# Overflow passes of two experts each in the MoE half of a two-layer decoder kernel, with the last group split the same way

## The reference

```python
def hier_moe(h, w_group, b_group, w_expert, b_expert, w_e_gate, w_e_up, w_e_down):
    t = h.reshape(-1, d)
    g_idx = jnp.argmax(t @ w_group + b_group, axis=-1)
    g_w = jnp.take_along_axis(jax.nn.softmax(g_logits, axis=-1), g_idx[:, None], axis=-1)
    e_in = jnp.take_along_axis(e_logits, g_idx[:, None, None], axis=1)[:, 0]
    top_v, top_i = lax.top_k(e_in, TOP_K)                      # TOP_K = 2 of 4
    top_w = jax.nn.softmax(top_v, axis=-1) * g_w
    hid = jax.nn.silu(jnp.einsum('td,edf->tef', t, w_e_gate)) * jnp.einsum('td,edf->tef', t, w_e_up)
    out = jnp.einsum('tef,efd,te->td', hid, w_e_down, combine.astype(t.dtype))
```

## Time and profile before

| | |
|---|---|
| median of 3 runs | 784.68 us |
| profiled execution | 784.63 us |
| its span, first to last instruction | 782.9 us |
| mean granted clock of TensorE (share of full) | 0.999 |
| PE busy | 772.4 us, 99% |
| DVE busy | 646.9 us, 83% |
| ACT busy | 508.1 us, 65% |
| moved by DMA | 186.76 MB |

### The profile page before, as it was taken

The page is one execution under the profiler, slowest core; times in us unless marked ns, Lnnn a source line. Parts: engine busy times, 40 slices in busy tenths (PEclk is TensorE's granted clock), DMA queues, the critical chain, the costliest instruction groups (busy, mean ns, idle before and its releaser), DMA issues.

```text
span 782.9 us, 13142 instructions
## 1 busy us (share of the span) xinstructions
PE 772.4 (99%) x4850; PEld 690.5 (88%) x4850; DVE 646.9 (83%) x847; ACT 508.1 (65%) x592; POOL 22.6 (3%) x36
## 2 busy tenths in 40 slices
PE   8999999999999999999999999999999999999997
PEld 7899999999878888888889999999988888888885
DVE  5868898469689999897874799757968998989895
ACT  7625646655588778786643655565569877878772
POOL 4020000000000000000001000000000000000000
PEclk9999999999999999999999999999999999999999
DMA  9867254266719999998365624526562999999971
GB/s 303 273 215 241 83 201 137 94 216 216 269 54 328 346 383 335 386 338 276 119 214 204 225 97 173 162 72 239 212 234 90 334 365 386 336 363 352 354 262 54
DMA packets 79499, 186.76 MB, mean 239 GB/s; under 512 B 12470, under 2 KB 24408, under 8 KB 79448
## 3 DMA queue, kind: packets, MB, share of 16 engines
q1 hardware_dynamic: 79448, 186.08, 67.0%
HBM read 185.01 MB, written 1.05 MB: 238 GB/s over the span
## 4 chain that ended last, share of the span: by engine, by line
PE 96%; DVE 1%; ACT 1%; DMA 1%; issue 1%; POOL 0%; DVEq 0%; SPq 0%; ACTq 0%; POOLq 0%
PE bank L1380 28%; PE bank L1382 28%; PE bank L1381 28%; PE bank L1774 2%; PE bank L1685 2%; PE bank L1800 1%; PE bank L1662 1%; PE bank L1539 1%; DMA x<-in_x 1%; PE bank L1445 1%; PE bank L1448 0%; PE bank L1560 0%; PE bank L1564 0%; PE bank L1655 0%; PE bank L1769 0%
## 5 line engine op out<-in xcount | busy, mean ns | idle before, releaser
L839 DVE TENSOR_TENSOR w_lo<-raw,w_hi 128x2048 fp32r<-128x2048 f32 (+1 forms) x144 | 313.5, 2197 | 56.4 <-ACT w_hi L522 55.8
L522 ACT ACTIVATE w_hi<-raw 128x2048 fp32r<-128x2048 f32 (+1 forms) x144 | 264.1, 1844 | 135.3 <-PE bank L1382 131.4
L1380 PE MATMUL bank<-a_hi,w_hi 128*128 128x256 f32 x688 | 195.8, 285 | 0.6 <-DVE a_lo L905 0.6
L1381 PE MATMUL bank<-a_hi,w_lo 128*128 128x256 f32 x688 | 194.6, 283 | 0.0
L1382 PE MATMUL bank<-a_lo,w_hi 128*128 128x256 f32 x688 | 194.6, 283 | 0.0
L1380 PE MATMUL bank<-w_hi,y_lo 128*128 128x512 f32 x432 | 170.9, 395 | 0.0
L1382 PE MATMUL bank<-w_lo,y_lo 128*128 128x512 f32 x432 | 168.6, 390 | 0.0
L1380 PEld LDWEIGHTS bank<-a_hi,w_hi 128*128 128x128 f32 x688 | 131.9, 192 | 1.6 <-issue 1.5
L1381 PEld LDWEIGHTS bank<-a_hi,w_lo 128*128 128x128 f32 x688 | 132.0, 192 | 0.1
L1382 PEld LDWEIGHTS bank<-a_lo,w_hi 128*128 128x128 f32 x688 | 132.0, 192 | 0.0
L1381 PE MATMUL bank<-w_hi,y_hi 128*128 128x512 f32 x288 | 112.3, 390 | 0.0
(11 more groups left out here) (309 smaller groups left out, 970.4 us busy)
## 6 DMA issues: line engine op xcount, KB each, us to landing
raw<-in_w_e_gate SPq DMA_DIRECT2D x63, 512.0 KB, 4.9
raw<-in_w_e_up SPq DMA_DIRECT2D x63, 512.0 KB, 6.5
raw<-in_w_gate SPq DMA_DIRECT2D x56, 512.0 KB, 4.5
mid<-in_w_e_down SPq DMA_DIRECT2D x54, 512.0 KB, 6.1
raw<-in_w_in SPq DMA_DIRECT2D x32, 512.0 KB, 6.6
raw<-in_w_e_down SPq DMA_DIRECT2D x18, 512.0 KB, 5.0
raw<-in_w_branch SPq DMA_DIRECT2D x16, 512.0 KB, 4.1
raw<-in_w_o SPq DMA_DIRECT2D x16, 512.0 KB, 4.4
```

Source lines behind the costliest of these rows:

```text
L522: a.activation(w_hi[:, at.part(n), 0:w], raw_at(slot)[:, 0:w], ACT.Copy).then_inc(hi_done, 1)
L839: v.tensor_tensor(w_lo[:, part, 0:w], raw_at(slot)[:, 0:w], w_hi[:, part, 0:w].bitcast(F32), ALU.subtract).then_inc(split_done, 1)
L1380: mm(ps, a2[0], b2[0], start=first, stop=False, skip_group_check=shared)
L1381: mm(ps, a2[1], b2[0], start=False, stop=False, skip_group_check=shared)
```

## The change: half passes for the overflow and for the fourth group

A **half pass** serves two experts of a group (6 units, `units_h`). Groups 0 to 2 keep full passes. Then come the half passes: those for an overflow, if there is one, then experts 12 and 13 of the fourth group, and last, written out, experts 14 and 15. All counters stay as for a full pass: a half pass adds what is missing (`SKIP`) at one of its units.

The tokens of the second 128 whose two best experts are the first two of their group form a class of their own, and are ranked behind all other tokens of the group. DVE finds the class from the expert logits, PE ranks with two masks (`ca`) instead of one, and counts twice: all tokens of the group, and those outside the class. If the first count is over 128, a half pass with the group's experts 0 and 1 is added; if the second is, another with 2 and 3.

Each unit of a half pass is loaded by four DMAs of 256 KB instead of two of 512 KB, with contiguous runs of 2 KB instead of 4 KB. Passes 1 and 2 are written out on PE, ACT and DVE, and the loop runs over half passes. The diff, cut to its core:

```diff
+    units_h = [("gu", 0, 0), ("gu", 0, 1), ("gu", 1, 0), ("gu", 1, 1), ("down", 0, 0), ("down", 1, 0)]
+    PART_H = (0, 1, 2, 3, 1, 2)
+    SKIP = NM - len(units_h)
...
+            return PART_H[n] if self.half else n % PART
+
+        def counted(self, n):
+            return self.unit(n) + 1 + (SKIP if self.half else 0)
+
+        def count(self, n):
+            return 1 + SKIP if self.half and n == 0 else 1
...
+            def load_half(at, l, e0):
+                for n, (kind, i, h) in enumerate(units_h):
+                    slot = at.raw(n)
+                    sp.wait_ge(split_done, at.free(n, False))
+                    dst = raw_at(slot)
+                    for j in range(2):
+                        for q in range(2):
+                            o = 1024 * j + 512 * q
+                            if kind == "gu":
+                                d = dst[:, o:o + 512].rearrange("p (c f) -> p c f", c=2)
+                                w = (w_e_gate, w_e_up)[j]
+                                s = w[l, e0 + i].rearrange("(p c) f -> p c f", c=KT)[:, 4 * h + 2 * q:4 * h + 2 * q + 2, :]
+                            else:
+                                d = dst[:, o:o + 512]
+                                s = w_e_down[l, e0 + i, P * j:P * j + P, 512 * q:512 * q + 512]
+                            sp.dma_start(d, s).then_inc(landed[slot], 16)
...
-                npass = sp.value_load(tab[0:1, 0, 6:7], min_val=NG, max_val=NG + 1)
-                with sp.Fori(NG - 1, npass) as p:
-                    g = sp.value_load(tab[0:1, 0, bass.ds(p, 1)], min_val=0, max_val=NG - 1)
-                    at = At(l, before + p, True)
-                    for n, (kind, i, h) in enumerate(units_m):
-                        load(at, n, kind, i, h, l, g * EPG + i)
-
+                lastp = sp.value_load(tab[0:1, 0, 7:8], min_val=NG, max_val=MAXP - 1)
+                with sp.Fori(NG - 1, lastp) as p:
+                    e0 = sp.value_load(tab[0:1, 1, bass.ds(p, 1)], min_val=0, max_val=NE - 2)
+                    load_half(At(l, before + p, True, True), l, e0)
+                load_half(At(l, before + lastp, True, True), l, NE - 2)
+                npass = sp.value_load(tab[0:1, 0, 8:9], min_val=NG + 1, max_val=MAXP)
...
+                def half_pass(at, PP, tile_next, next_slot, final):
...
+                    hi(at, 3)
+                    silu(0)
+                    hi(at, 4, at.unit(0) + PART + 2)
+                    hidden(0)
+                    hi(at, 5, at.unit(0) + PART + 3)
+                    silu(1)
+                    if not final:
+                        pass_tokens(0, next_slot)
+                        pass_tokens(1, next_slot)
+                        act.wait_ge(S("sil_done"), EPG * PP + EPG)
+                        a.activation(rcur, rslot[:, tile_next], ACT.Copy).then_inc(S("rcur_done"), 1)
+                    if not final or l < DEPTH - 1:
+                        hi(ahead, 0, at.unit(0) + PART + 1)
+                    hidden(1)
+                    if not final or l < DEPTH - 1:
+                        hi(ahead, 1, at.unit(0) + PART + 5)
+                    result(at, PP)
+                    if not final:
+                        hi(ahead, 2, at.unit(0) + PART + NM)
 
...
+                lastp = act.value_load(tab[0:1, 0, 7:8], min_val=NG, max_val=MAXP - 1)
+                expert_pass(At(l, before + 1, True), before + 1, slice(2, 3), 2 * P, False)
+                tile_next = act.value_load(tab[0:1, 0, 3:4], min_val=0, max_val=NG - 1)
+                expert_pass(At(l, before + 2, True), before + 2, bass.ds(tile_next, 1), tile_next * P, False, True)
+                with act.Fori(NG - 1, lastp) as p:
+                    tile_next = act.value_load(tab[0:1, 0, bass.ds(p + 1, 1)], min_val=0, max_val=NG - 1)
+                    half_pass(At(l, before + p, True, True), before + p, bass.ds(tile_next, 1), tile_next * P, False)
+                half_pass(At(l, before + lastp, True, True), before + lastp, None, None, True)
...
-                    step.do(v.tensor_reduce(gm[:, t:t + 1], lg[:, t, 0:NG], AX, ALU.max))
+                    best = step.mark(v.tensor_reduce(gm[:, t:t + 1], lg[:, t, 0:NG], AX, ALU.max))
+                    if t:
+                        e_t = lg[:, t, NG:NR].rearrange("p (g e) -> p g e", g=NG)
+                        step.mark(v.tensor_tensor(cl[:, 0, :], e_t[:, :, 2], e_t[:, :, 3], ALU.max))
+                        step.mark(v.tensor_tensor(cl[:, 1, :], e_t[:, :, 0], e_t[:, :, 1], ALU.min))
+                    step.upto(best)
                     step.do(v.scalar_tensor_tensor(out=r4[:, 0, t, :], in0=lg[:, t, 0:NG], scalar=gm[:, t:t + 1],
...
+                    step.mark(v.tensor_reduce(r1[:, 1, t:t + 1], r4[:, 0, t, :], AX, ALU.max))
+                    if t:
+                        step.mark(v.tensor_tensor(cl[:, 2, :], cl[:, 1, :], cl[:, 0, :], ALU.is_ge))
+                        step.mark(v.tensor_tensor(cl[:, 3, :], cl[:, 0, :], cl[:, 1, :], ALU.is_gt))
+                    step.upto(step.n)
+                    if t:
+                        for i in range(2):
+                            v.scalar_tensor_tensor(out=ca[:, NG * i:NG * i + NG], in0=r4[:, 0, t, :], scalar=r1[:, 1, t:t + 1],
...
+                        dve.wait_ge(S("class_done"), T * (l + 1))
+                        step.do(v.tensor_tensor(r8, small_ps[:, RANK[t]:RANK[t] + 2 * NG], ca, ALU.mult))
+                        step.do(v.tensor_reduce(rk[:, t:t + 1], r8, AX, ALU.add))
...
+                    step.do(v.tensor_tensor(cnt[:, 0, :], cnt[:, 0, :], cnt[:, 1, :], ALU.add))
+                    step.do(v.tensor_scalar(cnt[:, 2:4, :], cnt[:, 0:2, :], float(P), None, ALU.is_gt))
+                    step.mark(v.tensor_reduce(tab_f[:, 1, 8:9], cnt[:, 2:4, :].rearrange("p i g -> p (i g)"), AX, ALU.add))
...
+                def half_pass(at, PP, tile, tile_next, weights, final):
...
+                    lo(at, 3)
+                    hidden(0)
+                    lo(at, 4)
+                    hidden_lo(0)
+                    lo(at, 5)
+                    hidden(1)
+                    if not final:
+                        pass_low(PP, 0, tile_next)
+                        pass_low(PP, 1, tile_next)
+                    hidden_lo(1)
+                    if not final or l < DEPTH - 1:
+                        lo(ahead, 0)
+                    dve.wait_ge(S("scattered"), PP)
+                    v.tensor_scalar(sel_t, posb[:, :], icol[:, tile], None, ALU.is_equal)
+                    if not final:
+                        lo(ahead, 1)
+                    result_lo(PP)
+                    if not final:
+                        lo(ahead, 2)
...
+                    ps = bank[small_bank][:, RANK[t]:RANK[t] + NG + NG * t]
+                    if t:
+                        pe.wait_ge(S("class_done"), T * (l + 1))
+                        mm(ps[:, 0:NG], ones[:, :], ca[:, NG:2 * NG], start=False, stop=False, skip_group_check=True)
+                    else:
+                        pe.wait_ge(S("goh_done"), T * l + 1)
+                    mm(ps, below[:, :], ca if t else r4[:, 3, 0, :], start=False, stop=True,
                        skip_group_check=True).then_inc(S("rank_done"), 1)
 
                 def count():
...
+                def half_pass(at, PP):
...
+                    def down(e, n):
+                        ready(at, n)
+                        pe.wait_ge(S("hd_lo_done"), EPG * PP + 2 * e + 2)
+                        wp = parts(at, n, "p (c m) -> p c m", c=FT)
+                        for h in range(2):
+                            if e and h:
+                                last.then_inc(S("y_bank"), 1)
+                            for f in range(FT):
+                                last = three(bank[4 + h][:, :], both(HD_, e, f), both(wp, f, slice(512 * h, 512 * h + 512)),
+                                             e == 0 and f == 0, e == 1 and f == FT - 1)
+                        last.then_inc(unit_used, 1 + SKIP if e else 1)
+
+                    gate_up(0, 0, 0)
+                    gate_up(0, 1, 1)
+                    gate_up(1, 0, 2)
+                    hidden_tp(0)
+                    gate_up(1, 1, 3)
+                    pe.wait_ge(S("selt_done"), PP)
+                    down(0, 4)
+                    hidden_tp(1)
+                    for i in range(4):
+                        last = scatter(i)
+                    last.then_inc(S("scattered"), 1)
+                    down(1, 5)
...
-                npass = pe.value_load(tab[0:1, 0, 6:7], min_val=NG, max_val=NG + 1)
-                with pe.Fori(1, npass) as p:
-                    expert_pass(At(l, before + p, True), before + p, False)
+                lastp = pe.value_load(tab[0:1, 0, 7:8], min_val=NG, max_val=MAXP - 1)
+                npass = pe.value_load(tab[0:1, 0, 8:9], min_val=NG + 1, max_val=MAXP)
+                expert_pass(At(l, before + 1, True), before + 1, False)
```

(40 more changed lines are left out.)

198 lines of the change are left out of this document (112 added, 86 removed).

## The result

The changed kernel took **773.55 us** in the median of four runs (772.57 to 774.75), the kernel before 784.77 on the same chip (784.68 to 787.08): a ratio of 0.985, 95% interval 0.984 to 0.987. The forecast was 772.9 us with a range of 771.4 to 777.5.

The account below looks back on a forecast made before the run. TensorE, busy 99% of the span and 96% of the chain, was taken as the bound. +3.8 - 16.8 + 1.2 = -11.8 us against 784.63 gave 772.8, so a median of 772.9 us, range 771.4 to 777.5.

Parts of the forecast that it names:

- Step 1: Fourth group as two half passes in both layers: one more scatter each, +1.9 us per layer, +3.8 us.
- Step 2: Layer 1's overflow: the fifth full pass (35.47 us) gives way to one half pass (18.7 us), -16.8 us.
- the rival priced at 791.6: Layer 1's overflow needs both halves, so a second half pass adds 18.7 us: 791.6 us, slower; chance 3%.
- Step 3: Router, second 128 tokens: added DVE and PE work that nothing covers delays the select 0.6 us per layer, +1.2 us.
- the first pair: Two independent short DVE instructions added in the router before the group's one-hot: +0.2 us.
- The second pair: Two more DVE instructions before the group's one-hot in the router, for which the next has to wait: +0.25 us.
- Step 4: DVE and ACT in half passes: DVE needs 17.6 of 18.7 us and still fits, 0 us, at most 1.0 each.
- the rival of a late DVE: DVE delivers late in the half passes, up to 1.0 us in each of five: 773 to 778 us; chance 17%.
- Step 5: Weight transfers in half passes: 24 of 256 KB at 337 GB/s still keep up with six units buffered, 0 us.

Follow-up runs that it names:

- e4: Changed kernel with the fourth group a full pass again, now last, overflow half passes before it behind a branch: 768.98 us.
- e1: Changed kernel with the class made empty, so layer 1's overflow takes two half passes: 794.42 us, one run.
- e2: Changed kernel with class instructions, masks and second rank product removed from the router, overflow in two half passes: 790.02 us, one run.
- e7: Changed kernel with the router's two class comparisons moved ahead of the reduction to r1: 775.93 us, median of 4 runs.
- e5: Changed kernel with two unused 128x512 DVE sums added per half pass, ahead of the first expert's product: 775.73 us, one run.
- e6: Changed kernel with four unused 128x512 DVE sums added per half pass, ahead of the first expert's product: 785.52 us, one run.
- e3: Changed kernel with gate and up transfers of half passes in 512-byte runs instead of 2 KB, same bytes: 774.3 us, one run.

## Why the prediction was right

**The sum.** Forecast -11.8 us of span, found -12.1 once the fall of the clock is taken off, -10.6 with it in the profiled execution. The forecast of 772.9 lies 0.65 us below 773.55. That the median came so near is in part luck: the forecast had nothing for a fall of the clock, two of the four runs had one of 1.5 us, and the sum itself erred by 0.3 the other way. The terms are another matter; the experiments took them one by one.

**Step 1, the fourth group.** +3.8 forecast, +3.73 measured by taking it back (e4). The half pass of 18.7 us was 18.64 to 18.73.

**Step 2, the overflow.** -16.8 forecast. Layer 1 has -14.90 in its passes, of which +1.90 are the split: -16.80. That one half pass serves it rested on counts from the reference (132 and 115 against 128). e1 and e2 show the other branch of it: a second half pass 18.70 us long, the rival priced at 791.6; e2's 788.2 + 1.8 around it + 1.0 for the class is 791.0. The gain hangs on this routing: with a class too small to hold the four tokens that do not fit, the change is slower than the kernel before, as e1 is.

**Step 3, the router.** +1.2 forecast, 0.6 in each layer; +0.52 and +0.50 found against the kernel before (layer 1 by e4, 298.37 - 297.87), and +0.52 and +0.51 in the chains of e2. The walk to it had wrong pieces, and two of them cancelled. From L1159 to the one-hot L1165 it was 0.91 us before, and from L1234 to L1253 it is 1.35: +0.44 where I had +0.75. I took 0.14 us for an independent short instruction; in the rows above L1236 and L1239 start 0.07 us apart, and L1242, with L1240 between, 0.15 after L1239, so the first pair cost 0.03 and not 0.2. The second pair, costed at 0.25, can be read from 594.55, the start of the reduction L1244, to 594.88, the masks: 0.33 us where a dependent step has 0.19, so 0.14, and e7 gets 0.12 of it back. The masks take 0.27 of the 0.3 I gave them. What followed cost less than nothing in my walk (-0.15) and +0.07 in fact (1.87 us from L1253 to L1267, 1.80 before): PE has one product more to do after 595.29, and DVE's L1260 stood 0.22 us for the rank. Two errors of opposite sign, -0.31 and +0.22, and so the sum was close: that is luck. The Trainium skill (Perfetto Trace Analysis, "Optimizing Scalar/DVE Operations") puts the fixed cost of a DVE instruction on SBUF at about 60 ns, and says that the latency a profile shows is about twice that, since its second half overlaps with the next. By this the trace agrees: 0.07 us apart, 0.16 long.

**Step 4, DVE and ACT.** 0 forecast, 0 found: no wait of PE for the expert products. The walk gave a margin of 0.4 to 0.5 us at the tightest places; at the first expert's product it is 0.57 in the mean (e5, e6), 0.9 behind a full pass and 0.1 between two half passes, which the walk did not tell apart. The sum of DVE was 17.6 forecast; the windows have 16.88 to 17.70. So the rival of a late DVE was nearer than the forecast said: some 0.1 us more of DVE work there would have begun to show. By the mean margin it is an estimate that 3.0 us more per half pass (12.1 / 5 + 0.57) would have taken all of the gain. e6, with 2.38 added, has a span of 782.4 us, 0.5 below the kernel before; 2.4 of it are two falls of the clock in the router's stretches (its first scatter is 1.21 us late, and the stretch between the layers 1.22 longer than e4's).

**Step 5, transfers.** 0 forecast, 0 found, and e3's quarter-length runs cost nothing either. The issues of the changed kernel (count, KB each, median us from issue to landing):

```profile
raw<-in_w_e_gate SPq DMA_DIRECT2D x42, 512.0 KB, 4.5
...
raw<-in_w_e_gate SPq DMA_DIRECT2D x40, 256.0 KB, 4.5
```

Half the bytes of a gate land as late as the whole; the up transfers take 5.5 us against 6.2, the down transfers 4.9 against 5.9. So the time to landing follows the size far less than in proportion, as it would if most of it were the wait for those issued before; that cause is argued, not shown. Landing that late, 24 of them still fit in 18.64 us, so they overlap. The Trainium skill (DMA: Bandwidth & Descriptors, "Anatomy of one DMA"), which the prediction quoted, has 2.0 us fixed for each DMA, measured there on those issued from GpSimd. The prediction's estimate from it, some 200 us more if none overlapped, did not come: these are issued from SyncE, and they overlap.

**What the forecast did not say** is that a cheaper form of the same idea was open: the fourth group was split although its own tokens gain nothing by it, which takes back 3.7 of the 16.8 us. The cost stood in the prediction as step 1; that it is needless is in e4. The changed program never gives its loop over half passes an empty range (it starts at `NG - 1` and its end is at least `NG`), and half passes of the fourth group are what fills it in layer 0. e4's branch around the loop makes them unnecessary, and cost nothing on PE.

## What to carry to other kernels

Where one engine is 96% of the chain, count its instructions by kind, take each kind's pace from starts in the trace, and an edit of passes can be priced to a tenth of a microsecond. Ask of each part of a change on its own whether it pays: here one part gave 16.8 us and another took 3.7. To learn how near the next engine is, load it with two doses of idle work at one place; both must give the same margin. Then read the cost pass by pass: the mean here was 0.57 us, the tightest pass had 0.1.

## What the runs showed of the hardware that was not expected

- The clock granted to TensorE fell to 0.50 for some 3 us while PE showed as busy, in some executions and not in others. In four traces it fell at one place of the mixers, behind 5.5 us of small matmuls (near 466 in the changed kernel and e3; near 96 and 467 in e1 and e7), in e6 at two other places, amid the router's gathers (near 222 and 598). What decides whether it falls stays open. Each fall cost 1.2 to 1.5 us, more than the router's whole change, and a median of few runs moves with it. One run of the kernel before, beside the last four experiments, took 791.86 us at a mean clock of 0.989.
- The mean busy share of the DMA engines can stand at 1.06 to 1.16 in a stretch (four of e3's five half passes) with no later landing that PE feels, so it is not read as a ceiling of 1.00.
- Short independent DVE operations start 0.07 us apart and show 0.16 each; sums over 128x512 start 0.60 apart and show 0.68 each.
- An engine's slack is not the same in equal passes: the same 1.19 us of added DVE work cost 0.28 us in the first half pass behind a full one and 1.06 in one between two half passes (e5).
